# Where the split moving operands of a 1-core encoder trunk begin in SBUF: high parts at column 0, `hid` tiles 2304 bytes apart, both operands at a multiple of 256 bytes

## What is computed

```
h = concat(meta, x)
layer 0: h += concat(fourier_mix(u), conformer_conv(v)) @ W_out,   [u | v] = rms_norm(h) @ W_in
layer 0: h += relu(rms_norm(h) @ W1)^2 @ W2                        (2048 -> 8192 -> 2048)
layer 1: h += (B * dwconv3(C * h_in)) @ W_out,                     [B | C | h_in] = rms_norm(h) @ W_in
layer 1: h += relu(rms_norm(h) @ W1)^2 @ W2
out = rms_norm(h)[:, 16:, :]
```

## Time and profile before

| what | value |
|---|---|
| median of 3 runs | 2116.27 us (2115.98 to 2116.4) |
| the profiled execution, its own time | 2116.13 us |
| its span, first to last instruction | 2114.1 us |
| TensorE matmul busy | 2089.6 us, 15226 matmuls |
| VectorE, ScalarE busy | 1281.1 us, 927.1 us |
| granted TensorE clock | 0.998 of full speed |

### The profile page before, as it was taken

How to read it: one execution, slowest core, us unless ns; L and a number is a source line. 1 busy time by engine, 2 the same in 40 slices (tenths; PEclk the granted TensorE clock), 3 DMA queues, 4 the chain that set the end, 5 groups by cost and what they waited for, 6 DMA issues and landing times.

```text
span 2114.1 us, 36370 instructions
## 1 busy us (share of the span) xinstructions
PE 2089.6 (99%) x15226; PEld 1985.3 (94%) x15226; DVE 1281.1 (61%) x1300; ACT 927.1 (44%) x965; POOL 66.1 (3%) x40
## 2 busy tenths in 40 slices
PE   8999999999999999999999999999999999999997
PEld 8999999999999999999999999888888888888886
DVE  8999975545554554556566556665556555555555
ACT  6434464334434443445433334545335434434443
POOL 1001020000000000000100000010000000000001
PEclk9999999999999999999999999999999999999999
DMA  7442455555555555554555455455554554554552
GB/s 283 178 160 101 162 185 192 179 181 187 188 180 179 183 189 183 179 180 177 196 183 179 179 189 189 168 202 187 187 191 179 198 181 178 197 188 178 193 195 80
DMA packets 55336, 383.91 MB, mean 182 GB/s; under 512 B 6176, under 2 KB 8224, under 8 KB 9312
## 3 DMA queue, kind: packets, MB, share of 16 engines
q1 hardware_dynamic: 54880, 381.84, 50.1%
q0 software_dynamic: 240, 1.02, 0.1%
q10 hardware_dynamic: 144, 0.04, 0.0%
HBM read 380.78 MB, written 2.10 MB: 181 GB/s over the span
## 4 chain that ended last, share of the span: by engine, by line
PE 96%; DVE 2%; ACT 1%; issue 0%; DMA 0%; DVEq 0%; SPq 0%
PE banks L310 25%; PE banks L304 20%; PE banks L302 19%; PE banks L303 19%; PE banks L311 13%; DVE wl L796 1%; ACT wh L519 0%; DVE h L824 0%; ACT xs L536 0%; DMA raw<-weights 0%; DVE ssum L935 0%; DVE h L1149 0%; DVE h L1155 0%; ACT sq L546 0%; PE banks L437 0%
## 5 line engine op out<-in xcount | busy, mean ns | idle before, releaser
L796 DVE TENSOR_TENSOR wl<-raw,wh 128x1024 fp32r<-128x1024 f32 x720 | 891.9, 1249 | 720.6 <-ACT wh L519 719.5
L519 ACT ACTIVATE wh<-raw 128x1024 fp32r<-128x1024 f32 x720 | 753.9, 1058 | 971.3 <-PE banks L304 610.9
L302 PE MATMUL banks<-xs,wh 128*128 128x258 f32 (+1 forms) x2176 | 618.3, 284 | 10.3 <-DVE wl L796 10.3
L304 PE MATMUL banks<-xs,wl 128*128 128x258 f32 (+1 forms) x2176 | 621.1, 285 | 0.0
L303 PE MATMUL banks<-xs,wh 128*128 128x258 f32 (+1 forms) x2176 | 614.3, 282 | 0.0
L310 PE MATMUL banks<-hid,wh 128*128 128x512 f32 x1280 | 448.5, 395 | 0.0
L302 PEld LDWEIGHTS banks<-xs,wh 128*128 128x128 f32 x2176 | 412.4, 190 | 10.6 <-issue 8.8
L303 PEld LDWEIGHTS banks<-xs,wh 128*128 128x128 f32 x2176 | 411.4, 189 | 0.1
L304 PEld LDWEIGHTS banks<-xs,wl 128*128 128x128 f32 x2176 | 409.9, 188 | 0.0
L304 PE MATMUL banks<-hid,wl 128*128 128x258 f32 x1280 | 363.8, 284 | 0.0
L302 PE MATMUL banks<-hid,wh 128*128 128x258 f32 x1280 | 361.9, 283 | 1.4 <-DVE hid L840 1.4
(11 more groups left out here) (103 smaller groups left out, 779.5 us busy)
## 6 DMA issues: line engine op xcount, KB each, us to landing
raw<-weights SPq DMA_DIRECT2D x359, 1024.0 KB, 4.8
out<-h SPq DMA_DIRECT2D x8, 256.0 KB, 2.7
h<-x SPq DMA_DIRECT2D x3, 544.0 KB, 10.6
raw<-weights SPq DMA_DIRECT2D x2, 512.0 KB, 6.0
conv<-dft_seq POOLq DMA_DIRECT2D x1, 580.5 KB, 13.2
h<-x SPq DMA_DIRECT2D x2, 272.0 KB, 4.3
act<-dft_ch POOLq DMA_DIRECT2D x1, 258.0 KB, 7.9
par<-params POOLq DMA_DIRECT2D x1, 160.0 KB, 6.4
```

The costliest lines, as they stand in the source:

```text
L302: pe.matmul(dst, w[0], v[0], start=start, stop=False)
L304: return pe.matmul(dst, w[1], v[0], start=False, stop=stop)
L519: act.activation(wh[:, j % RING, :, :], src.rearrange("p (t c) -> p t c", t=SLAB_K), ACT.Copy).then_inc(high_ready, 1)
L796: dve.tensor_tensor(wl[:, j % RING, :, :], src.rearrange("p (t c) -> p t c", t=SLAB_K), wh[:, j % RING, :, :].bitcast(F32), ALU.subtract). ...
```

## The change

The high part of a tile now begins at column 0 of the tile. The low part begins right behind it where both fit a stream of 512 columns (lo = 16), otherwise at column 272 as before. `hid` gets tiles of 576 columns, 2304 bytes, nine times 256; those of `xs` stay 2176 bytes apart, eight and a half times 256. `hid` now comes ahead of `xs`, and an unused tensor of 128 bytes, `to_line`, lies between `h` and `hid`, so that `hid`, and behind it `xs`, begin at a multiple of 256 bytes. Everything behind `xs` (`raw`, `wh`, `wl` and the rest) moves by 2176 bytes. No instruction is added or removed.

```
+HID_PITCH = 576
...
         h = sb("h", [P, KT, L])
+        to_line = sb("to_line", [P, 32])
+        hid = sb("hid", [P, KT, HID_PITCH], F32R)
         xs = sb("xs", [P, KT, 2 * L], F32R)
-        hid = sb("hid", [P, KT, 2 * L], F32R)
...
         def high_of(t, tile, lo):
-            return t[:, tile, lo:L]
+            return t[:, tile, 0:L - lo]
 
         def low_of_tile(t, tile, lo):
-            return t[:, tile, L:2 * L - lo]
+            at = L - lo if 2 * (L - lo) <= COLS else L
+            return t[:, tile, at:at + L - lo]
 
         def both_of(t, tile, lo):
-            return t[:, tile, lo:2 * L - lo]
+            return t[:, tile, 0:2 * (L - lo)]
```

## The result

The change made the kernel slower: 2126.87 us, median of five runs (2126.45 to 2127.17), against 2115.98 us (2114.93 to 2116.4). The ratio is 1.0052, 95% interval 1.004 to 1.0064, 10.9 us. I had forecast 2105 us, faster, with a range up to 2126; the time lies 0.9 us above the range, and it went the other way. The nearest of my cases was rival C (2132 us).

A forecast was written before the change was run, and what follows sets the result against it. TensorE's matmul stream was taken as the bound; -7.7 - 5.1 + 1.4 = -11.4 us from 2116.2 gave 2104.8, forecast as 2105 us, 0.5% faster, with a range of 2088 to 2126.

The forecast's parts named there:

- rival C: Stream starts count against the weights' start, so every hid stream turns dear: +16 us, 2132 us, chance 0.19.
- What bounds the kernel: TensorE's matmul stream, busy 99% of the span; only the distance between matmul starts can move the time.
- The classes: Tiles with parts beginning at 0 and 64 (modulo 256) cost 8 ns less than those at 128 and 192.
- Part 1: hid at lo = 14, layer-0 output and first MLP: all tiles cheap, -6 ns on 1280 triples, -7.7 us.
- Part 2: hid at lo = 16, layer-1 output and second MLP: all streams begin at 0, -4 ns on 1280 pairs, -5.1 us.
- Part 3: xs at lo = 14, first MLP and layer-1 input, 1792 triples: half the tiles stay dear, +1.4 us.
- Part 4: xs at lo = 0 and lo = 16: one tile of each class stays, 0, with a bound of -10 us.
- Part 5: The weights wh and wl move from 128 to 0 modulo 256: 0 claimed.
- Rival A: The total hangs on nothing here, since the excess is 12 ns for both mixes: 2116 us, chance 0.28.

The follow-up runs named there:

- layout alone: The changed kernel with the three helpers as before, so high parts again at column lo: 2121.86 us, ratio 1.0029 to the kernel before.
- second probe: Computation left out, 67 matmul streams in the kernel's order with own tile distances and starts: 358.2 ns a tile for the layout before, 366.7 for changed hid.
- the search: Computation left out, 60 layouts each streamed twice, after different neighbours: 46 gave the same distance within 0.5 ns; 258 columns from 353.3 to 366.7, 370.0 at worst.

## Why the prediction was wrong, point by point

**What bounds the kernel** held. TensorE's stream is the bound in every kernel here, nothing but the distance of matmuls moved, and the copies without any other engine have the kernels' distances, but for one that settled at the other of its two rates.

**The classes** failed, and with them all that was built on them. I took a tile's time for a property of its own address modulo 256, cheap at 0 and 64, dear at 128 and 192. I had named the other reading, the offset from the weights, and moving the weights alone showed that this is the right one: the tiles changed places. Counted from the weights of the kernel before, my cheap starts were offsets 128 and 192, and the change put the hid parts at offsets 0 and 64. And I read the classes off the stages of 272 and 512 + 256 columns and used them for 258, where the trace of the kernel before has them the other way round: 355.2 ns for the even tiles, my dear class, 361.7 for the odd ones. The prediction never reads the tiles of that stage, and it is the one that decided.

**Part 1**, hid with 258 columns, is the step that cost most: -7.7 us predicted, +9.7 measured (1.2 + 8.5). A stretch of 100 us on hid was to hold 15 matmuls more than one on xs; it holds 11 fewer. The flaw is deeper than the wrong reference point. I assumed that a tile keeps its price when its neighbour changes. It does not: the even tiles before, high and low 56 and 64 behind the weights, took 355.2 ns between odd ones; a stream of only such tiles takes 360.0 (layout alone, and L81 of the probe). The price belongs to the sequence of offsets that repeats, not to its members. The measured +8.3 ns a triple in MLP 1 lies at my upper bound of +8, but by luck: the bound was the price of the dear class at 272 columns.

**Part 2**, hid with 512 + 256: -5.1 predicted, -2.9 measured (-3.2 and +0.3), right in sign, and the sign that I had named for being right, records that no longer alternate, came true on hid. The reason given was wrong, though: against the weights these streams begin at 0, an offset that no stream of 512 had before, and that rival C counted as dear. Offset 64 everywhere, the layout alone, is indeed dear at 353.3.

**Part 3**, xs with 258: +1.4 predicted, +7.0 measured. I carried the excess of the first stage's mix over to 258 columns. At the same offsets 272 columns gave 36.8 ns above the columns, and 258 give 362.3 - 322.5 = 39.8. The price depends on the length too.

**Part 4** held for the first stage; on xs in MLP 2 I had 0, with a bound of -10, and it gave -1.6.

**Part 5**, the weights: 0 is right for the sum of the kernel before (2115.59), whose even and odd tiles changed places. It is no rule: the copy of the changed hid pairs ran at 353.3 ns with the weights at 0 and at 351.0 with the weights 128 bytes on (L83 and L94 of the second probe).

**Rival A** had the strongest argument, and it is instructive why it fell. The excess was 12 ns for two mixes, and 120.6 in the DFT. These were three of the many patterns; the 60 of the search show that 258 columns can take 353 to 370 ns a tile, and the mean of many patterns is near the one I had. Agreement of a few samples was no law. Of the Trainium skill's 16-byte lines ("SBUF — State Buffer", "Specifications (TRN2)") the runs show that they don't account for these differences: in the second probe columns 14 and 288 of a hid tile, 353.3 ns (L99), and 14 and 272, 360.0 (L81), touch the same number of such lines. **Rival C** had the right reference point, the weights, and the wrong prices. Its terms add up to 16.7, not 16. The hid pairs, +5.1 in it, gave -2.9; the xs triples, +1.4, gave +7.0; xs at 512 + 256 and the first stage, 0, gave -2.4. That these errors leave its sum only 5 us too high is luck in part, as is its +10.2 for the hid triples, from the same bound as above.

The range ended 0.9 us short. With C at 0.19 I cut it at half of C's way, and the bounds of the parts, +10.2 and +5.1, would have held the result.

## What to carry to other kernels

Where TensorE streams float32r operands without a gap, as here, the start of the moving part against the stationary part, modulo 256 bytes, is worth up to 4% of a stage, in either direction, and rounding the starts of tiles and weights to a multiple of 256 is no safe choice: here it was among the worst for 258 columns. A price read off one count of columns doesn't hold for another. Don't infer the price of a new layout from single matmuls of an old one; stream the whole repeating sequence in a small probe (12 us a layout), try several, and check the winner in the kernel, since some layouts settle in more than one way. With changes of many tensors at once, move one alone: shifting the weights by 128 bytes changed no time and told more than any run that did.

## What the runs showed of the hardware that I had not expected

- Many repeating sequences settle on lengths that are whole multiples of 16 columns' time, 6.67 ns: 366.7, 360.0, 353.3 and 346.7 ns a tile are 55, 54, 53 and 52 of them, the 358.3 of the layout before is 215 over four tiles. Of the 120 streams of the search 59 lie within 0.13 ns of a whole multiple a tile and 28 of a half one; for the rest it is not shown.
- A stream of 512 float32r columns came at 226.8 to 233.3 ns, never at its 213.3, even with nothing else running and with 32 stationary columns (231.7). In the Trainium skill, "TensorE: Matmul & The Clock Gate", section "Back-to-back issue gap", N / 2.4 + 2.5 for an isolated matmul gives an estimate of 215.8; the plain float32 matmuls keep to 2.5 above their two passes, the float32r ones miss it by 11 to 18.
- One layout can hold two rates in the same kernel: 353.3 and 346.7 ns a tile for hid pairs of the changed kernel, with the change at an interruption of the stream. Columns 14 and 288 of hid did it between programs, 353.3 in both probes and 356.7 in the kernel. What selects a rate was not found, and not tried beyond the second entry of each layout in the search.
